# Second feed-forward: the last two groups of the down projection, for three of the four quarters of the hidden layer, as seven block products

## What is computed

```
f = jnp.square(jax.nn.relu(h @ w_ffn_up[i])) @ w_ffn_down[i]      # first_block, then x + rms_norm(f)
x = x + jnp.square(jax.nn.relu(h @ w_up[l])) @ w_down[l]          # second_block
```

## Time and profile before

| what | us |
|---|---|
| median of 3 runs | 1257.31 (1255.83 to 1258.53) |
| the profiled execution, its own time | 1255.79 |
| its span, first to last instruction | 1253.9 |
| TensorE busy in the span | 1226.7 (98%) |
| VectorE, ScalarE, GpSimd busy | 766.6, 590.2, 399.2 |
| mean granted clock of TensorE | 0.999 |

### The profile page before, as it was taken

The page is one execution under the profiler, slowest core; times in us unless marked ns, Lnnn a source line. Parts: engine busy times, 40 slices in busy tenths (PEclk is TensorE's granted clock), DMA queues, the critical chain, the costliest instruction groups (busy, mean ns, idle before and its releaser), DMA issues.

```text
span 1253.9 us, 26624 instructions
## 1 busy us (share of the span) xinstructions
PE 1226.7 (98%) x11269; PEld 1128.2 (90%) x11269; DVE 766.6 (61%) x1049; ACT 590.2 (47%) x1036; POOL 399.2 (32%) x314
## 2 busy tenths in 40 slices
PE   8999999998999999999999999999999999999998
PEld 7777797787999999999999997776899999999997
DVE  5678746566468339468376567434584594673863
ACT  4555536456355346246155454544442362451642
POOL 7022236332005136235252232000051462443510
PEclk9999999999999999999999999999999999999999
DMA  6223300001432323323334233122233234232331
GB/s 200 68 67 101 101 2 3 3 3 62 144 102 93 110 68 102 115 88 105 99 101 135 70 111 98 35 67 85 67 101 102 68 105 129 70 123 80 102 119 67
DMA packets 102075, 108.88 MB, mean 87 GB/s; under 512 B 1971, under 2 KB 97253, under 8 KB 101958
## 3 DMA queue, kind: packets, MB, share of 16 engines
q1 hardware_dynamic: 101878, 106.93, 27.2%
q0 software_dynamic: 80, 0.26, 0.1%
HBM read 105.08 MB, written 2.10 MB: 85 GB/s over the span
## 4 chain that ended last, share of the span: by engine, by line
PE 90%; DVE 5%; ACT 3%; issue 1%; POOL 1%; DVEq 0%; POOLq 0%; ACTq 0%
PE ps L556 11%; PE ps L558 11%; PE ps L557 11%; PE ps L647 6%; PE ps L648 6%; PE ps L649 6%; PE ps L520 4%; PE ps L522 4%; PE ps L521 4%; PE ps L607 2%; PE ps L609 2%; PE ps L608 2%; PE ps L1186 1%; PE ps L1188 1%; PE ps L1187 1%
## 5 line engine op out<-in xcount | busy, mean ns | idle before, releaser
L556 PE MATMUL ps<-w_hi,a_hi 128*128 128x256 f32 x1024 | 286.0, 279 | 0.0
L557 PE MATMUL ps<-w_lo,a_hi 128*128 128x256 f32 x1024 | 285.8, 279 | 0.0
L558 PE MATMUL ps<-w_hi,a_lo 128*128 128x256 f32 x1024 | 285.8, 279 | 0.0
L556 PEld LDWEIGHTS ps<-w_hi,a_hi 128*128 128x128 f32 x1024 | 192.5, 188 | 0.1
L557 PEld LDWEIGHTS ps<-w_lo,a_hi 128*128 128x128 f32 x1024 | 192.5, 188 | 0.1
L558 PEld LDWEIGHTS ps<-w_hi,a_lo 128*128 128x128 f32 x1024 | 192.5, 188 | 0.0
L1919 DVE TENSOR_TENSOR w_lo<-w_raw,w_hi 128x2048 fp32r<-128x2048 f32 (+1 forms) x55 | 130.1, 2365 | 72.4 <-ACT w_hi L1276 72.2
L1276 ACT ACTIVATE w_hi<-w_raw 128x2048 fp32r<-128x2048 f32 (+1 forms) x55 | 104.4, 1899 | 133.4 <-PE ps L558 108.1
L2840 POOL TENSOR_TENSOR hsq<-tmp 128x512 f32<-128x512 f32 x64 | 95.0, 1500 | 88.9 <-ACT tmp L1388 62.2
L2025 DVE TENSOR_TENSOR w_lo<-w_raw,w_hi 128x1024 fp32r<-128x1024 f32 (+1 forms) x72 | 95.1, 1334 | 25.8 <-ACT w_hi L1349 25.6
L647 PE MATMUL ps<-th,w_hi 128*128 128x256 f32 x384 | 108.1, 281 | 0.4 <-ACT tmp L1374 0.4
(11 more groups left out here) (419 smaller groups left out, 3090.6 us busy)
## 6 DMA issues: line engine op xcount, KB each, us to landing
w_raw<-w_ffn_up_dram SPq DMA_DIRECT2D x16, 1024.0 KB, 5.6
w_raw<-w_ffn_down_dram SPq DMA_DIRECT2D x16, 1024.0 KB, 5.1
w_raw<-w_up_dram SPq DMA_DIRECT2D x16, 1024.0 KB, 5.6
w_raw<-w_down_dram SPq DMA_DIRECT2D x16, 1024.0 KB, 5.2
w_raw<-w_in_first_dram SPq DMA_DIRECT2D x12, 1024.0 KB, 5.4
w_raw<-w_out_dram SPq DMA_DIRECT2D x8, 1024.0 KB, 5.2
xn<-x_dram SPq DMA_DIRECT2D x8, 512.0 KB, 5.9
w_raw<-w_in_dram SPq DMA_DIRECT2D x4, 1024.0 KB, 6.5
```

The source lines that it names most:

```text
L556: mm(o, hi[:, hb + k, tok], whi, start=first and own and k == ks[0], stop=False, skip_group_check=True)
L557: mm(o, hi[:, hb + k, tok], wlo, start=False, stop=False, skip_group_check=True)
L558: m = mm(o, lo[:, hb + k, tok], whi, start=False, stop=last and k == ks[-1], skip_group_check=True)
```

## The change

It does five things.

1. **Seven blocks.** For b = 1 and q = 0 to 2 (`paired`), down groups c = 2 and 3 are taken together by a new function `seven_down`: seven products of 24 matmuls each (168 in place of 192), in PSUM banks 4 to 6, with seven additions to `xn` in place of four. The contraction and the tokens are cut in two.
2. **Weight sums.** VectorE makes the four sums of down weights (`sum_down`, 128x1024 each, into `D1`, `D2`, in place, `D4`), and the seven blocks are split one by one (`upper_down` on ScalarE, `lower_down` on VectorE).
3. **Sums of the squares.** GpSimd makes four sums of 128x256 for each up group of these quarters (`sums_dt`), ScalarE and VectorE split the result (`upper_down_t`, `lower_down_t`, four of 128x1024 each).
4. **Squares.** In b = 1 the float32 squares move from GpSimd to ScalarE, right behind `square_high`, into two buffers by turns (`hsq`, `squares_odd`). Those of b = 0 stay on GpSimd, but the first of them stands behind t4 in its list now.
5. **Loads and buffers.** The first load of the next quarter also waits for the four weight sums. `block_free` and the tile numbers follow.

The diff, cut to what is spoken of, engine by engine: SyncE, TensorE, ScalarE (`square_high` and `ffn`), VectorE, GpSimd. `before_last` is `lower_block` of the next quarter's A11, `before_end` those of its SUM2 and SUM1:

```diff
+                    if u == 0 and q and paired(b, q - 1):
+                        sp.wait_ge(sm["d_sum"], 4 * q)
...
+            def seven_down(q):
...
+                pe.wait_ge(sm["db_lo"], down_at(q, A11))
+                one(A11, 0, True)
+                pe.wait_ge(sm["w_lo_ready"], g + 1)
+                one(A12, 1, True)
+                pe.wait_ge(sm["db_lo"], down_at(q, SUM2))
+                pe.wait_ge(sm["dt_lower"], 4 * q + 4)
+                pe.wait_ge(sm["tile_evacuated"], tile + 1)
+                one(SUM2, 0, False)
+                pe.wait_ge(sm["db_lo"], down_at(q, SUM1))
+                one(SUM1, 2, True)
+                pe.wait_ge(sm["db_lo"], down_at(q, SUM3))
+                pe.wait_ge(sm["tile_evacuated"], tile + 3)
+                one(SUM3, 0, False)
+                pe.wait_ge(sm["db_lo"], down_at(q, SUM4))
+                pe.wait_ge(sm["tile_evacuated"], tile + 4)
+                one(SUM4, 2, False)
+                pe.wait_ge(sm["w_lo_ready"], g + 2)
+                pe.wait_ge(sm["tile_evacuated"], tile + 5)
+                one(A22, 0, False)
...
-            def square_high(u, j):
+            def square_high(b, q, u, j):
                 act.drain()
                 af(a_hi[:, 2 * u + j, :], tmp[:, 2 * (u % 2) + j, :], ACT.Square).then_inc(sm["a_ready"], 1)
+                if b == 1:
+                    act.wait_ge(sm["squared"], square_at(b, q, u) + j + 1)
+                    if 4 * q + u > 1:
+                        act.wait_ge(sm["dt_sum"], min(4 * q + u - 1, 12))
+                    af(square_slot(b, u, j), tmp[:, 2 * (u % 2) + j, :], ACT.Square).then_inc(sm["square_f32"], 1)
...
+                    if paired(b, q):
+                        for t in (1, 0, 2, 3):
+                            upper_down_t(q, t)
+                        for x in (A11, A12, SUM2, SUM1, SUM3, SUM4, A22):
+                            upper_down(q, x)
+                        upper_a(b, q + 1, 0)
+                        upper_sum(b, q + 1, 0, SUM2)
+                        upper_sum(b, q + 1, 0, SUM1)
+                        continue
...
+            def seven_down(q, before_last, before_end):
+                lower_down(q, SUM2)
+                lower_down(q, SUM1)
+                add_product(q, A11, 0, 0, 0)
+                lower_down(q, SUM3)
+                dve.drain()
+                add_product(q, A12, 1, 0, 0)
+                lower_down(q, SUM4)
+                add_product(q, SUM2, 0, 1, 0)
+                lower_down(q, A22)
+                add_product(q, SUM1, 2, 1, 1)
+                before_last()
+                dve.drain()
+                add_product(q, SUM3, 0, 1, 1)
+                dve.drain()
+                before_end()
+                add_product(q, SUM4, 2, 1, 0)
+                add_product(q, A22, 0, 0, 1)
...
+            def sums_dt(q, u):
+                pool.wait_ge(sm["square_f32"], square_at(1, q, u) + 2)
...
+                g_.tensor_tensor(t1, x[:, high], x[:, low], ALU.subtract)
+                g_.tensor_tensor(t3, y[:, high], x[:, high], ALU.subtract)
+                pool.drain()
+                g_.tensor_tensor(t2, y[:, high], t1, ALU.subtract)
+                pool.drain()
+                g_.tensor_tensor(t4, y[:, low], t2, ALU.subtract).then_inc(sm["dt_sum"], 1)
...
                 g_.tensor_tensor(t3, t3, h_lo[:, 0:KH, 2 * P:4 * P].bitcast(F32), ALU.subtract).then_inc(sm["t_pool"], 1)
-                square_f32(b, 0, 0, 0)
                 pool.wait_ge(sm["t_sum"], 3 * b + 3)
                 g_.tensor_tensor(t4, h_hi[:, KH:KT, 0:2 * P].bitcast(F32), tf1[:, 1], ALU.subtract)
                 pool.drain()
                 g_.tensor_tensor(t4, t4, h_lo[:, KH:KT, 0:2 * P].bitcast(F32), ALU.add).then_inc(sm["t_pool"], 1)
-                square_f32(b, 0, 0, 1)
...
+                if b == 1:
+                    for u in range(4):
+                        sums_dt(0, u)
+                else:
+                    square_f32(b, 0, 0, 0)
...
                        if u < 3:
                            last_sum(b, q, u + 1)
-                        if u:
+                        if u and paired(b, q):
+                            sums_dt(q, u - 1)
+                        if u and b == 0:
                             square_f32(b, q, u - 1, 0)
                             square_f32(b, q, u - 1, 1)
                         if u < 2:
                             sums_s(b, q, u + 2)
```

More of the change, by code:

```diff
@@ L311, in done @@
         def done(g):
-            return 2 * g + 5 * sum(group(b, q, u) < g for b in range(2) for q in range(4) for u in seven(q))
+            return (2 * g + 5 * sum(group(b, q, u) < g for b in range(2) for q in range(4) for u in seven(q))
+                    + 3 * sum(group(1, q, 7) < g for q in range(3)))
         def block_free(b, q, u, n):
             g = group(b, q, u)
+            if u == 0 and b == 1:
+                return done(g - 2) + {A11: SUM3, A12: SUM3, SUM2: SUM4, SUM1: SUM4, SUM3: A22, SUM4: A22, A22: SUM1}[n] + 1
             if u == 0:
@@ L330, in block_at, with paired, square_slot, down_block @@
             return 5 * seventh(b, q, u) + order.index(n) + 1
+        def paired(b, q):
+            return b == 1 and q < 3
+        def square_slot(b, u, j):
+            return (squares_odd if b and u % 2 else hsq)[:, j, :]
+        def down_block(w, n):
+            at_ = {A11: 4, A12: 6, SUM2: 0, SUM1: 2, SUM3: 4, SUM4: 6, A22: 0}[n] * S
+            return w[:, at_:at_ + 2 * S].rearrange("q (k n) -> q k n", n=GW)
+        def down_raw(q, part):
+            j, k = divmod(part, 2)
+            return w_raw[:, group(1, q, 6 + j) % 2, k::2, :]
+        def down_at(q, n):
+            return 5 * q + (A11, SUM2, SUM1, SUM3, SUM4).index(n) + 1
+        def down_upper_t(n):
+            if n < 2:
+                return (h_hi, h_lo)[n][:, 0:KH, 2 * P:4 * P]
+            return dt_hi[:, n - 2]
         def raw(g, part):
@@ L699, in ffn @@
                                 m.then_inc(sm["mm_done"], 1)
-                    for c in range(1, 4 if q < 3 else 2):
+                    for c in range(1, 4 if q < 3 and not paired(b, q) else 2):
                         natural_group(g + c, tile + 2 * c, 0, a_hi, a_lo)
+                    if paired(b, q):
+                        seven_down(q)
                 def bank(c, late):
@@ L2125, in up, with lower_down @@
                     square_low(b, q, u - 1, 1)
+            def lower_down(q, n):
+                g = group(1, q, 6)
+                if n in (A12, A22):
+                    dve.wait_ge(sm["w_hi_ready"], g + (1 if n == A12 else 2))
+                else:
+                    dve.wait_ge(sm["db_hi"], down_at(q, n))
+                src = {A11: down_raw(q, 0), A12: down_raw(q, 1), SUM1: D1[:, :, :], SUM2: D2[:, :, :], SUM3: down_raw(q, 2),
+                       SUM4: D4[:, :, :], A22: down_raw(q, 3)}[n]
+                v.tensor_tensor(down_block(block_lo, n), src, down_block(block_hi, n).bitcast(F32), ALU.subtract)\
+                    .then_inc(sm["w_lo_ready" if n in (A12, A22) else "db_lo"], 1)
```

136 lines of the change are left out of this document (122 added, 14 removed).

## The result

The changed kernel takes 1265.74 us (median of 6 runs, 1264.55 to 1269.68), the kernel before 1257.88 on the same chip (6 runs, 1255.83 to 1259.67). The ratio is 1.0072, 95% interval 1.0056 to 1.0088: slower by 7.9 us. The prediction had 1260.0 and a range up to 1265.0, so the direction was right and the size was not. The profiled execution of the changed kernel took 1265.77 us, 9.98 more than that of the kernel before.

A forecast was written before the change was run, and what follows sets the result against it. TensorE, busy 98% of the span, was taken to bound the kernel. Terms -8.4 + 1.8 + 2.3 + 0.3 + 6.2 + 0.5 = +2.7 gave 1258.5 us against the profiled execution, 1260.0 against the median; range 1256.0 to 1265.0.

The forecast's parts named there:

- Term 1: Down stages of three quarters: 24 fewer matmuls in each, 72 x 0.1167 us, -8.4.
- Term 2: Seven-block down stages: TensorE waits, chiefly 0.6 us in front of A22 in each of three quarters, +1.8.
- Loads: Next quarter's loads for groups 0 and 1 go out later but land in time: cost 0, 1.5 to 7 us cover.
- Term 3: First feed-forward: GpSimd's first square behind t4 delays the half weight that TensorE needs, +2.3.
- second feed-forward's start: Second feed-forward: first square on ScalarE behind the high one pushes everything after by 0.53; half weight later, +0.3.
- Term 4: Up stages of q = 1 and 2: GpSimd's four square sums delay ScalarE's third copy 3.1 us each, +6.2.
- Term 5: Up stages: ScalarE's two more squares a group fit; third copies of the last group 0.15 late, +0.5.
- the clock falls: Third rival: clock falls to 1.2 GHz at both Term 4 waits, 1.6 more each, +3.2: 1263.2; chance 0.12.
- Its own sign of being wrong: Whole kernel: the prediction is wrong if, among other signs, the clock row shows under 1.00 before the end.
- 0.2 of slack: Seven-block down stage: A11's result is added by 27.9, the third block in its bank starts at 28.1.
- ScalarE becomes the bound: Rival: both squares fall whole on the copies of groups 2 and 3, three quarters, +6.4 more, 1266; chance 0.10.
- GpSimd is in time: Rival: four square sums under 2.0 us let S2 reach ScalarE in time, Term 4 is 0: 1253.8; chance 0.08.

The follow-up runs named there:

- The VectorE order alone: Changed kernel with two additions of block results to `xn` moved earlier in VectorE's list in `seven_down`: 1262.18 us, ratio 1.0051 to the kernel before.
- the squares alone: Kernel before with only the b = 1 float32 squares moved to ScalarE with two buffers, no seven blocks or sums: 1260.59 us, ratio 1.0026.
- two smaller orders: Changed kernel with GpSimd's weight sums first, its first square back before t4, and VectorE's additions earlier, all together: 1253.17 us, ratio 0.9956.
- the weight sums first: Changed kernel with GpSimd's weight sums of group u+2 before the four square sums of group u-1: 1258.41 us, ratio 1.0000 to the kernel before.
- the first square back: Changed kernel with GpSimd's first square of the first feed-forward put back in front of t4: 1263.47 us, ratio 1.0036 to the kernel before.

## Why the prediction was wrong

| step of the prediction | predicted | in the profile |
|---|---|---|
| Term 1, 72 matmuls fewer | -8.4 | -8.4 |
| Term 2, the seven blocks' waits | +1.8 | +3.4 |
| Loads | 0 | 0 |
| Term 3, moved square | +2.3 | +2.3 |
| second feed-forward's start | +0.3 | +0.2 |
| Term 4, GpSimd's list | +6.2 | +6.3 |
| Term 5, ScalarE's squares | +0.5 | +1.3 |
| last down stage (q = 3) | 0 (not named) | +0.4 |
| the clock | 0 (a rival) | +4.7 |
| sum | +2.7 | +10.2 |

The right column is read from the starts of TensorE's matmuls; its sum is the difference of the spans, 1264.1 - 1253.9 = 10.2. Term 5 is what is left over in the up stages. Without the clock's row it is +5.5. Between the medians lie 7.9, so there the clock took about 7.9 - 5.5 = 2.4 (the profiled execution had a fall at 312 besides, which comes and goes without the change). The fit over the runs gives about the same from other data: 2.8 of a difference of means of 8.5, which leaves 5.7 for all else.

**What failed first** is the choice between the forecast and its third rival. The prediction gave 0.12 to "the clock falls" and took the clock at 1.00 in its sum, because the only fall in the trace of before was behind the last matmul. It priced a fall at 1.6, which is what the starts show; but it looked for falls behind term 4's waits only, and the 2.7 us wait of term 3 is long enough as well. With falls at seven in ten of three such waits the estimate is 0.7 x 3 x 1.6 = 3.4, above the 2.4 to 2.8 that were found. Its own sign of being wrong, a clock under 1.00 before the end, came true. The upper end of the range, 1265.0, is also 0.6 more than its own terms make (1263.2 + 1.2). The clock alone, some 2.8 on top of 1260.0, would have stayed inside that range; it took terms 2 and 5 as well.

**Term 2 was too small**, by 1.6. The wait in front of A22 is there with 0.54, 0.54 and 0.55, for 0.6; but VectorE's order put A11's addition late too. The "0.2 of slack" in front of the block that goes on in A11's bank was none in q = 1 and 2, where that block started 0.43 and 0.15 late (0.19 of idle time at 1069.32). And the step left out that a wait costs more than its idle time. From when it was due to its end the block A22 with 0.54 of wait takes 3.63 us for 2.80, the up product with 2.93 of wait 4.59 for 1.42: 0.29 and 0.24 more than the wait. The VectorE order alone took 3.6 off, 2.9 of them in these stages.

**Term 5 was too small**, by 0.8. It said that eight squares of 0.53 fit in 12 us of idle ScalarE. With the squares alone each up stage is 0.55 longer, about one square; idle time of the engine does not help a copy that stands behind a square in its queue. In the changed kernel 1.3 are left when term 4's waits and the clock's 1.6 are taken off the 9.2 by which the three up stages grew (43.41, 45.19 and 39.99 us for 39.80, 39.78 and 39.77). This is the rival "ScalarE becomes the bound" in small, not as priced (6.4). The last down stage lasts 51.51 for 51.10 us, with no wait to show for it; why stays open.

**Term 4 and term 3 were right in place, size and chain.** The four sums took 5.14 for 5.2; the copy came 2.93 late for 3.1; line 573 waited 2.67, where 2.5 to 2.7 was named. The loads were right too: in the down stage that starts at 1040.87 the two went out 24.9 and 33.9 us in, for 24.4 and 34.5, and landed 5.7 and 5.6 later, and no matmul waits behind them. The rival "GpSimd is in time" falls with the same rows. The assumed durations, GpSimd's four sums and VectorE's weight sums, have rows now (from 870 us on, by line and shape):

```profile
L3067 POOL TENSOR_TENSOR dt_f<-squares_odd,dt_f 128x256 f32<-128x256 f32 x6 | 11.2, 1867 | 0.9
...
L3069 POOL TENSOR_TENSOR dt_f<-squares_odd,dt_f 128x256 f32<-128x256 f32 x6 | 4.4, 739 | 0.8
...
L2289 DVE TENSOR_TENSOR hn_odd<-w_raw 128x1024 f32<-128x1024 f32 x3 | 3.7, 1222 | 0.0
```

The 0.74 read off the line through 512 and 1024 columns is the 739 ns, the 1.22 taken from the low part is the 1222 ns. The other group shows what company does to the same instruction: 1867 ns in the mean, between 0.75 and 2.63 us singly.

The Trainium skill (SBUF — State Buffer, Who interferes with whom) says that a VectorE instruction with two inputs in SBUF contends with a GpSimd instruction that reads SBUF, and that the shared ports are an exclusive lock. The trace agrees in single instructions. In these rows VectorE's instruction ends at 1049.50 and the sum, begun beside it, only at 1050.10, after 2.62 us for 0.74 alone:

```profile
1047.21 2.29 DVE L2056 TENSOR_TENSOR w_lo<-w_raw,w_hi 128x2048 fp32r<-128x2048 f32 x1 [0.47 <-ACT w_hi L1380]
...
1047.48 2.62 POOL L3067 TENSOR_TENSOR dt_f<-squares_odd,dt_f 128x256 f32<-128x256 f32 x1
```

## What to carry to other kernels

Before work is added to an engine's hand-written queue, write down when each result behind it is due: here the same four sums cost 6.3 us in front of the two weight sums and 0.6 behind them. That order alone brings a change that loses 7.9 us back to even, and with two smaller orders put right it gains 4.9. An engine that is busy for a third of the span, as GpSimd here, can still hold all others when a step that waits stands in front of what is due. A wait of TensorE of some 2.7 us is to be booked with more than its length: 0.2 to 0.3 us of restart each, and in seven of ten cases here about 1.6 of lower clock, once twice that.

## What the runs showed of the hardware

- A wait of TensorE costs 0.24 to 0.29 us beyond the idle time that its row shows (3.63 for 2.80 with 0.54, 4.59 for 1.42 with 2.93).
- A fall of the granted clock to 0.50 moves the matmuls behind it by 1.5 to 1.6 us where (1 - clock) x time is 1.7. At waits of 2.67 to 2.94 us there was one in seven of ten, one of the seven twice as long (399 us in the kernel with the weight sums first); at the wait of 5.16 one that was twice as long too (0.50 for three stretches, 0.91 and 0.88 beside them). At 1.94 us there was one in five of nine, at 1.69 in two of nine.
- The same wait is followed by a fall in one execution and not in another: the one that ends between 1025 and 1029 with the first square back and with VectorE's order, but not in the changed kernel; the one near 1115 in the changed kernel and with the first square back, but not with VectorE's order. So one profile cannot tell whether a wait is followed by a fall; the mean clock over the runs can.
